# Two-pass matmuls of 256 columns, activations at another distance from the weight rings, low parts piece by piece

## What is computed

```python
# first block
z = rms_norm(h, g) @ w_in                       # q, k, v, u, gate input
h = h + concat(diff_attention(q, k, v), u * spatial(layer_norm(vg))) @ w_out
f = rms_norm(h, g);  h = h + (silu(f @ ffn_w1) * (f @ ffn_w3)) @ ffn_w2      # hidden 5632
h = h + (p @ pl_w_up) * sigmoid(h @ pl_w_gate)
# second block, 16 meta tokens ahead of the 256
proj = rms_norm(h, g) @ w_in_2                  # u, gb, gc, v, two gates
y_a = (pool(u) @ pool_w) * pool_scale
y_b = (gb * causal_conv(gc * v)) @ conv_out_w
h = h + (sigmoid(ga) * y_a + sigmoid(gbr) * y_b) @ w_o
h = h + (silu(gate) * up) @ w_down              # hidden 5632
out = rms_norm(h, g)
```

## Time and profile before

| | |
|---|---|
| median of 3 runs | 2665.51 us |
| the profiled execution | 2665.68 us |
| its span | 2663.6 us |
| TensorE busy | 2652.8 us (100%) |
| weight loads (PEld) | 2347.5 us (88%) |
| VectorE (DVE) | 1658.5 us (62%) |
| ScalarE (ACT) | 1236.0 us (46%) |
| mean granted TensorE clock | 0.999 |
| read from HBM | 498.37 MB, 188 GB/s over the span |

### The profile page before, as it was taken

One profiled execution on the slowest core, in us unless ns is written; L12 is line 12 of the kernel. 1 busy time (PEld: TensorE's weight loads), 2 busy tenths in 40 slices (PEclk: granted clock), 3 DMA queues, 4 the chain that ended last, 5 costly groups with the idle time before them and its releaser, 6 DMA issues.

```text
span 2663.6 us, 39872 instructions
## 1 busy us (share of the span) xinstructions
PE 2652.8 (100%) x15711; PEld 2347.5 (88%) x15711; DVE 1658.5 (62%) x1645; ACT 1236.0 (46%) x1355; POOL 0.8 (0%) x7
## 2 busy tenths in 40 slices
PE   9999999999999999999999999999999999999998
PEld 8889888888888888888999999888888888888887
DVE  6567766555565556795676666556765645564555
ACT  5456554444444444565443443444554434443444
POOL 0000000000000000000000000000000000000000
PEclk9999999999999999999999999999999999999999
DMA  8554555655656555555555555555565555565553
GB/s 291 184 174 145 195 189 193 193 193 188 198 181 205 181 199 189 185 191 191 176 175 189 181 184 182 190 182 190 189 205 189 189 189 189 189 198 192 180 192 138
DMA packets 254251, 502.92 MB, mean 189 GB/s; under 512 B 8130, under 2 KB 11652, under 8 KB 253988
## 3 DMA queue, kind: packets, MB, share of 16 engines
q1 hardware_dynamic: 252180, 497.61, 56.6%
q10 hardware_dynamic: 1952, 3.68, 0.4%
HBM read 498.37 MB, written 2.88 MB: 188 GB/s over the span
## 4 chain that ended last, share of the span: by engine, by line
PE 99%; DVE 0%; ACT 0%; DMA 0%; issue 0%; ACTq 0%; DVEq 0%
PE ps L1359 49%; PE ps L1373 24%; PE ps L1392 4%; PE ps L1394 4%; PE ps L1393 4%; PE ps L1412 4%; PE ps L1411 4%; PE ps L1410 3%; PE ps L1403 0%; PE ps L1402 0%; PE ps L1404 0%; PE ps L1322 0%; DMA xtok<-in_x_dram 0%; PE ps L1547 0%; PE ps L1545 0%; PE ps L1546 0%
## 5 line engine op out<-in xcount | busy, mean ns | idle before, releaser
L825 DVE TENSOR_TENSOR lo<-raw,hi 128x1024 fp32r<-128x1024 f32 x940 | 1127.8, 1223 | 852.2 <-ACT hi L491 843.6
L491 ACT ACTIVATE hi<-raw 128x1024 fp32r<-128x1024 f32 x940 | 971.5, 1055 | 1061.2 <-PE ps L1373 483.6
L1359 PE MATMUL ps<-A,hi 128*128 128x512 f32 x3648 | 862.8, 393 | 0.0
L1359 PEld LDWEIGHTS ps<-A,hi 128*128 128x128 f32 x3648 | 675.6, 188 | 140.4
L1359 PE MATMUL ps<-B,hi 128*128 128x512 f32 x1984 | 477.5, 394 | 0.0
L1373 PEld LDWEIGHTS ps<-A,lo 128*128 128x128 f32 x3648 | 438.0, 188 | 12.0
L1373 PE MATMUL ps<-A,lo 128*128 128x256 f32 x3648 | 439.9, 277 | 0.0
L1359 PEld LDWEIGHTS ps<-B,hi 128*128 128x128 f32 x1984 | 365.3, 188 | 74.8
L1373 PEld LDWEIGHTS ps<-B,lo 128*128 128x128 f32 x1984 | 246.1, 188 | 10.0
L1373 PE MATMUL ps<-B,lo 128*128 128x256 f32 x1984 | 247.8, 279 | 0.0
L1412 PE MATMUL ps<-B,lo 128*128 128x258 f32 (+1 forms) x768 | 219.4, 286 | 0.0
(11 more groups left out here) (240 smaller groups left out, 1342.6 us busy)
## 6 DMA issues: line engine op xcount, KB each, us to landing
raw<-in_w_in_dram SPq DMA_DIRECT2D x136, 1024.0 KB, 5.1
raw<-in_ffn_w_dram SPq DMA_DIRECT2D x132, 1024.0 KB, 5.1
raw<-in_w_gate_up_dram SPq DMA_DIRECT2D x88, 1024.0 KB, 5.0
raw<-in_w_down_dram SPq DMA_DIRECT2D x44, 1024.0 KB, 5.1
raw<-in_w_out_dram SPq DMA_DIRECT2D x16, 1024.0 KB, 5.2
raw<-in_pl_w_gate_dram SPq DMA_DIRECT2D x16, 1024.0 KB, 5.1
raw<-in_conv_out_w_dram SPq DMA_DIRECT2D x16, 1024.0 KB, 5.1
raw<-in_w_o_dram SPq DMA_DIRECT2D x16, 1024.0 KB, 5.1
```

The lines of the kernel that those rows point to most:

```text
L491: act.activation(hi[:, slot % RING], raw[:, raw_slot, 2 * (slot % 2):2 * (slot % 2) + 2, :], ACT.Copy).then_inc(hi_ready, 1)
L825: dve.tensor_tensor(lo[:, slot % RING], raw[:, slot // 2 % RAWS, 2 * (slot % 2):2 * (slot % 2) + 2, :], hi[:, slot % RING], ALU.subtract). ...
L1359: last = pe.matmul(ps[:, b0 + m, :], high(slot, kk, m), both, start=j == 0 and kk == 0, stop=ends and j == seg.pieces - 1 and kk == 1)
```

## The change

It has four parts.

1. `highs` multiplies each high tile twice with 256 columns, first four tiles with the high activations and then the same four with the low ones, all into the first half of the bank. `pieces_used` is raised by `lows` alone.
2. The pairs and `SNAKED` go: each piece runs its high parts and then at once its low parts.
3. The copy of the second half goes on ScalarE, and the adding of the halves on VectorE. The group's own step on VectorE reads the banks itself once the whole group is done (`sums_done`), and it releases them (`free_sums`); ScalarE waits for that release (`wait_group`) where it waited for VectorE's hand-over. The semaphore `copied` goes, with its tally.
4. The 128 bytes of ln_stats leave the place between hi and lo (it is 96 bytes now, behind sumsq), rstd_meta and tiny change places, and TOKEN_AT becomes 32. Modulo 256 bytes, from hi: lo at 0, A at 192, B at 128, the two-pass rows of B at 192, its token rows at 0.

```diff
-TOKEN_AT = META + 32
+TOKEN_AT = META + 16
...
         hi = sb("hi", [P, RING, 2, GC], F32R)
-        ln_stats = sb("ln_stats", [P, 32])
         lo = sb("lo", [P, RING, 2, GC], F32R)
 
+        rstd_meta = sb("rstd_meta", [P, META])
...
         tiny = sb("tiny", [P, 2, TM])
-        rstd_meta = sb("rstd_meta", [P, META])
...
+        ln_stats = sb("ln_stats", [P, 24])
...
-            before = [None]
-
-            def copy_second(kind, G, end, b0):
-
-                act.wait_ge(pieces_used, end)
-                act.wait_ge(psum_free, G)
-                if SQUARED & {kind, before[0]}:
-                    wait(ready)
-                before[0] = kind
-                act.activation(pb_copy[:, :, :], ps[:, b0:b0 + 4, T:2 * T], ACT.Copy).then_inc(copied, 1)
+            def wait_group(G):
+
+
+                act.wait_ge(psum_free, G + 1)
+                act.nop(nofuse=True)
...
-            def add_halves(G, b0, to):
-                second.skip()
-                wait(second)
+            def sums_done(end):
+
+                dve.wait_ge(pieces_used, end)
                 wait(given)
                 wait(ready)
-                dve.tensor_tensor(to, ps[:, b0:b0 + 4, 0:T], pb_copy[:, :, :], ALU.add).then_inc(psum_free, 1)
+
+            def free_sums(ins, G):
+
+                ins.then_inc(psum_free, 1)
                 dve.wait_ge(psum_free, G + 1)
...
                 elif kind == "qk":
-                    add_halves(G, b0, work[:, :, :])
-                    pe_in.mark(dve.tensor_tensor(qk[:, k:k + 4, :], work[:, :, :], Rm, ALU.mult))
+                    sums_done(end)
+                    free_sums(dve.tensor_tensor(qk[:, k:k + 4, :], sums, Rm, ALU.mult), G)
...
                 elif kind in ("gate", "ga", "gbr"):
-                    add_halves(G, b0, work[:, :, :])
-                    hand(dve.tensor_tensor(work[:, :, :], work[:, :, :], Rm, ALU.mult))
+                    sums_done(end)
+                    free_sums(dve.tensor_tensor(work[:, :, :], sums, Rm, ALU.mult), G)
...
-            def highs(seg, g, j, slot, b0, n, ends=False):
+            def highs(seg, g, j, slot, b0, n):
 
                 buf, layout, _ = seg.reads
                 X = activations(buf, layout)
+                at = 0 if layout == "halves" else META
                 pe.wait_ge(hi_ready, n + 1)
                 for kk in range(2):
                     k = 2 * j + kk + (4 * WIDEST_FIRST[g] if seg.name == "pool" else 0)
-                    for m in range(MT):
-                        both = X[:, k, 0:2 * T] if layout == "halves" else X[:, k, META:META + 2 * T]
-                        last = pe.matmul(ps[:, b0 + m, :], high(slot, kk, m), both, start=j == 0 and kk == 0,
-                                         stop=ends and j == seg.pieces - 1 and kk == 1)
-                if ends:
-                    last.then_inc(pieces_used, 1)
-
-            def lows(seg, g, j, slot, b0, n, ends=True):
+                    for part in range(2):
+                        x = X[:, k, at + part * T:at + (part + 1) * T]
+                        for m in range(MT):
+                            pe.matmul(ps[:, b0 + m, 0:T], high(slot, kk, m), x, start=j == 0 and kk == 0 and part == 0, stop=False)
+
+            def lows(seg, g, j, slot, b0, n):
 
                 buf, layout, _ = seg.reads
                 X = activations(buf, layout)
...
                     Xh = X[:, k, 0:T] if layout == "halves" else X[:, k, META:TM]
                     for m in range(MT):
                         last = pe.matmul(ps[:, b0 + m, 0:T], low(slot, kk, m), Xh, start=False,
-                                         stop=ends and j == seg.pieces - 1 and kk == 1)
-                if ends:
-                    last.then_inc(pieces_used, 1)
+                                         stop=j == seg.pieces - 1 and kk == 1)
+                last.then_inc(pieces_used, 1)
...
                         if hd == 0:
-                            v_in.skip(4)
                             wait(v_in)
+                            pe.wait_ge(psum_free, QK.g0 + 4)
...
                             if not two_passes(seg, g):
                                 piece(seg, g, j, slot, b0, n)
-                            elif seg.reads[1] in ("halves", "wide_halves") and j % 2 == 0 and j + 1 < seg.pieces and not beside:
-                                lows_first = j % 4 == 2 and seg.name in SNAKED
-                                for i in range(2):
-                                    if lows_first:
-                                        lows(seg, g, j + i, slot + i, b0, n + i, ends=False)
-                                    else:
-                                        highs(seg, g, j + i, slot + i, b0, n + i)
-                                together = True
-                            elif j % 2 and together:
-                                for i in range(2):
-                                    if lows_first:
-                                        highs(seg, g, j - 1 + i, slot - 1 + i, b0, n - 1 + i, ends=True)
-                                    else:
-                                        lows(seg, g, j - 1 + i, slot - 1 + i, b0, n - 1 + i)
-                                together = False
                             else:
                                 highs(seg, g, j, slot, b0, n)
                                 lows(seg, g, j, slot, b0, n)
```

More of the change, by code:

```diff
@@ L132 @@
 PER = {
[L133 to L136 removed]
+    "res_ffn": (2, 0, 2, 1), "part": (0, 0, 0, 0), "gate": (0, 0, 1, 0), "up": (0, 1, 1, 1),
+    "plgate": (5, 2, 4, 1), "ga": (0, 0, 1, 0), "gbr": (0, 0, 1, 0), "cv": (1, 0, 0, 0),
+    "cg": (5, 0, 0, 0), "cb": (0, 1, 1, 1), "cout": (0, 1, 1, 1), "res_ffn2": (3, 0, 2, 1),
+    "tpart": (0, 0, 0, 0),
 }
@@ L141 @@
         "cg": 1, "cb": 1, "cout": 1, "u2": 2, "cv": 0}
-SQUARED = {"res_ffn", "res_ffn2", "plgate"}
-SNAKED = {"qk", "out"} | {f"f{i}_{part}{c}" for i in (1, 2) for part in ("up", "down") for c in range(3)}
 SIDE = {
@@ L191, in turns_of @@
 def turns_of(eng, seg, tallies, run, lead=0):
-    per = [sum(PER.get(kind, (0,) * 5)[i] for kind in seg.kinds) for i in range(5)]
+    per = [sum(PER.get(kind, (0,) * 4)[i] for kind in seg.kinds) for i in range(4)]
     whole = seg.turns if seg.turns == 1 else min(seg.turns, max(seg.peel, lead))
@@ L390, in bass_two_blocks @@
         PLUP = next(s for s in SEGS if s.name == "plup")
+        QK = next(s for s in SEGS if s.name == "qk")
         def landed(n):
@@ L556, in evacuate @@
                     return
-                copy_second(kind, G, end, b0)
-                if kind not in ("qk", "plup", "pool"):
-                    more()
-                if kind in ("qk", "part", "plup", "pool"):
+                if kind in ("qk", "plup", "pool"):
+                    return
+                more()
+                if kind == "part":
                     return
                 if kind in ("res_ffn", "res_ffn2"):
-                    asked.skip()
-                    wait_alone(asked)
+                    wait(ready)
+                    wait_group(G)
                     given.mark(act.activation(pb_copy[:, :, :], some(h, k, 4, 0, T), ACT.Square))
@@ L892, in evacuate @@
                     hk = some(h, k, 4, 0, T)
-                    add_halves(G, b0, work[:, :, :])
-                    step(dve.tensor_tensor(hk, hk, work[:, :, :], ALU.add))
+                    sums_done(end)
+                    free_sums(dve.tensor_tensor(hk, hk, sums, ALU.add), G)
                     more()
                 elif kind == "res_gate":
-                    add_halves(G, b0, work[:, :, :])
+                    hk = some(h, k, 4, 0, T)
+                    sums_done(end)
+                    free_sums(dve.tensor_tensor(hk, hk, sums, ALU.add), G)
                     if gi < MT - 1:
@@ L909, in evacuate @@
                 elif kind in ("up", "cb"):
-                    add_halves(G, b0, work[:, :, :])
-                    step(dve.tensor_tensor(work[:, :, :], work[:, :, :], Rm, ALU.mult))
+                    sums_done(end)
+                    free_sums(dve.tensor_tensor(work[:, :, :], sums, Rm, ALU.mult), G)
                     if kind == "up":
@@ L918, in evacuate @@
                 elif kind == "cout":
-                    add_halves(G, b0, work[:, :, :])
-                    step(dve.tensor_tensor(work[:, :, :], work[:, :, :], some(G2, k, 4, 0, T), ALU.mult))
+                    sums_done(end)
+                    free_sums(dve.tensor_tensor(work[:, :, :], sums, some(G2, k, 4, 0, T), ALU.mult), G)
                     hand(dve.tensor_tensor(work[:, :, :], work[:, :, :], some(G1, k, 4, 0, T), ALU.add))
@@ L968, in evacuate @@
                 elif kind == "pool":
-                    add_halves(G, b0, work[:, :, :])
+                    sums_done(end)
                     for i in range(MT):
-                        last = dve.scalar_tensor_tensor(out=G1[:, k + i, :], in0=work[:, i, :], scalar=gain("pscale", k + i),
```

(5 more changed lines are left out.)

38 lines of the change are left out of this document (16 added, 22 removed).

## The result

| | before | after |
|---|---|---|
| median of 7 runs each | 2665.51 us | 2674.82 us |
| lowest to highest | 2665.26 to 2666.21 | 2674.70 to 2674.91 |
| ratio, 95% interval | | 1.0035 [1.0025, 1.0044] |

What follows compares the result with a forecast made beforehand. TensorE's matmul rate alone was taken to bound the kernel: 2665.7 us, less 27 for splitting the high matmuls and 1 for "u", all else zero, gave 2638 us; range 2614 to 2706, about 0.8.

Steps and rivals of the forecast that it cites:

- the 168: Two-pass pieces in segments counted as having the slower rate before, 2.815 us each; the other 540 counted at 2.740.
- Two steps: TensorE's 256-column matmuls start either 113.3 ns apart (short step) or 117.8 (long step); a step holds for long.
- rival 4: The new distance also lowers the least time of 256-column matmuls, to 110 ns: 56 us less, 2582 us; chance 0.03.
- rival 3: Two short matmuls for one long cost a fixed 2.3 ns per added matmul: 13 us more, 2679 us; chance 0.05.
- The price of splitting, -27 with the short step: 708 two-pass pieces as 24 matmuls of 256 columns: 1952.5 to 1925.8 us at 113.3 ns; +49 at 117.8.
- Which step?: Split two-pass stream: the uniform distance to both rings was taken, without proof, to favour 113.3 ns; bounds -27 and +49 us.
- Rival 2: A mixture of both steps, drawn at each of some ten entries to stretches: 2650 to 2700 us, centre 2672; chance 0.19.
- "u", -1: The "u" segment's 384 matmuls of 256 columns, between 113.2 and 118.9 ns, about half each before: 1 us less.
- The other segments, put at 0 between -18 and +17: u2, conv and token matmuls only change distance: 18 us less to 17 us more, taken as 0.
- Order within a piece, put at nothing: Lows directly behind highs: splits run three pieces ahead, so no added wait; a late piece would cost up to 2.3 us.
- Evacuation, put at nothing: ScalarE's copies (98 us) and VectorE's adds (113 us) go; TensorE waits for neither, so zero change in time.
- A fixed part for each matmul: The skill's 2.5 ns per matmul would make splitting cost 14 us more; the prediction said the trace disagrees.

## Why the prediction was wrong

- **What bounds.** Right. TensorE's rate alone moved the time: 99% of the chain is on it, its waits went from 2.9 to 3.4 us. The base of the sum was 2.7 us low: the two-pass matmuls of before took 1955.2 us, not 1952.5, because some pieces outside the 168 had the long step too.
- **Two steps.** Right, and to the number: 113.3 and 117.8 ns were taken from stretches of 18 to 32 matmuls; 17361 of them now lie at 113.35 and 117.78. No step of the changed kernel is below 113, so rival 4 has no support; a 512-column token matmul at 226.7 is twice 113.3, so rival 3 has none.
- **The price of splitting, -27 with the short step.** Right: without the layout part it measured -27.9 us, of which the two-pass matmuls have 27.4. That run has the new order and evacuation too.
- **"Which step? ... A uniform distance takes that irregularity away. I therefore take the short step."** This failed. I read the layout as evening out the stream. The runs show the reverse: in the split stream the unequal pair 64/192 ends nearly every long stretch within its first two pieces, and the uniform 192 lets one last for thousands, in one case for 6264 matmuls, to the end of plup. The part that I counted as the support of the gain cost it: 37.2 us between 2637.6 and 2674.8. What could have warned me stood in the earlier trace rows: in before low stretches ran at 192 with either step, so 192 by itself was shown to favour none. The sentence "a step once entered stays until the next stop" failed with it: at 64/192 the long step ends without a stop, and at 1101 us in the changed kernel it did too.
- **The draw.** Rival 2, a mixture between 2650 and 2700 with centre 2672, is what happened (2674.8). That it lies near the centre is luck: kernels with the same layout and a few transposes more took 2672.5 and 2648.2. I gave it 0.19 because I thought that the distance would bias the draw. Over the three kernels at 192/192 with 256 columns 9443, 8876 and 3245 matmuls are long.
- **"u", -1.** It gave 0.6 us: 117.0 to 115.5 ns in the mean.
- **The other segments, put at 0 between -18 and +17.** They gave -1.9 us: token -4.3, conv +1.7, u2 +0.7.
- **Order within a piece, put at nothing.** No wait for `lo` appeared, as said. It has a use that I had not seen, some 2 us at 64/192.
- **Evacuation, put at nothing.** Nothing speaks against it, though no run has it apart from the splitting. VectorE lost 86 us of busy time instead of 113 and ScalarE 64 instead of 98; 17 and 19 of the difference are in the splits, now 1144.7 and 990.6 us. No wait of TensorE went with them.
- **A fixed part for each matmul.** The least steps here are 113.3 ns for 256 columns and 226.7 for 512, twice as much, so there is none. The rule of the Trainium skill (TensorE: Matmul & The Clock Gate, Back-to-back issue gap), N/2.4 + 2.5 ns, gives 109.2 and 215.8 ns as an estimate; the page calls it the gap of a single matmul by itself, which the prediction left out. The measurement decides for this data type.

## What to carry to other kernels

Where one engine's stream is the bound, read its rate from start times, stretch by stretch, and ask of a layout which step each stretch will keep, not which it could have. A change of layout and a change of tiling belong in separate runs: here one was worth -28 us, the other +37 on top of it, and together they looked like a small loss. A kernel whose time moves by 27 us with a few added 0.1 us instructions has a step that is drawn, and a distance that ends the bad one is worth more than a lucky draw.

## What the runs showed of the hardware

- The step of float32r matmuls depends on the distance modulo 256 bytes between moving rows and weights; multiples of 64 were tried. For 256 columns, with both rings at the same distance: 120.0 ns at 0, 117.8 at 64, 118.6 at 128 and either 113.3 or 117.8 at 192. For 512-column highs: 227.9 in the mean at 0, 229.1 or 233.5 at 64 with lows at 192, 233.1 at 192. For the 512-column token matmuls that read A: 227.7 at 0, 233.3 at 64, 232.3 at 128, 230.2 at 192; for those that read B 226.7 at 0.
- A matmul's own distance doesn't settle it: 256-column highs at 64 take 117.8 ns where the lows are at 64, and 113.5 where they are at 0.
- At 192/192 the stream holds either of two steps over thousands of matmuls. One transpose turned chunk 1 from 117.8 to 113.3 ns, two left it at 117.8, and neither one nor two turned chunk 2.
- In the split stream at 64/192 the long step ended by itself, within 16 to 43 matmuls at most entries, in four kernels (625, 749, 910 and some 640 long ones of 17361 recorded). In "u" and around plup and the transposes it lasted for up to 194.
- The step does not follow the other engines. In one window of the first FFN, 384 to 1005 us, VectorE was busy for 325.6 us at the long step and 338.6 at the short one, DMA at 0.57 and 0.59: they follow TensorE's pace, at a granted clock of 1.00 in both.
- Which circuit makes the two steps stays open.
